# Two heads' score products side by side, and the gate products moved into the attention, in a two-block transformer kernel

## The reference, cut to what matters

```
mod = silu(c) @ w_ada + b_ada ; mod_c = silu(c_ctx) @ w_ada + b_ada
hx, hc = modulate(rmsnorm(x)), modulate(rmsnorm(ctx))
qa, ka, va, qb, kb, vb, ga, gb = project(hx)      # w_in, heads of 64, q and k normed per head
ka, va, kb, vb of hx (with rotary embedding) and of hc are concatenated: 512 keys
ya = softmax(qa ka^T / 8) va                      # 8 query heads, 2 key heads (grouped)
yb = (softmax(q1 k1^T / 8) - lam * softmax(q2 k2^T / 8)) vb    # 4 heads, two halves of 64 each
yb = rmsnorm(yb per head) * subln * 0.8
x  = x + g_a * ((sigmoid(ga) * (ya @ w_oa) + sigmoid(gb) * (yb @ w_ob)) @ w_out)
x  = x + g_m * moe(modulate(rmsnorm(x)))          # router, 32 experts, top 4
```

## Time and profile before

| | |
|---|---|
| median of 3 runs | 2022.0 us (2020.96 to 2022.55) |
| span of the profiled execution | 2021.8 us |
| first block up to the expert loop | 0 to 412.4 us |
| of it: projections / second part of the modulation / attention | 46.3 to 202 / 202 to 231 / 231 to 319.5 us |
| expert loop | 412.4 to about 1425 us |
| TensorE busy | 1822.9 us, 90% |

### The profile page before, as it was taken

One profiled execution on the slowest core, in us unless ns is written; L12 is line 12 of the kernel. 1 busy time (PEld: TensorE's weight loads), 2 busy tenths in 40 slices (PEclk: granted clock), 3 DMA queues, 4 the chain that ended last, 5 costly groups with the idle time before them and its releaser, 6 DMA issues.

```text
span 2021.8 us, 18937 instructions
## 1 busy us (share of the span) xinstructions
PE 1822.9 (90%) x7644; PEld 951.9 (47%) x7644; DVE 379.6 (19%) x806; ACT 318.8 (16%) x612; POOL 35.5 (2%) x35
## 2 busy tenths in 40 slices
PE   4999868799989899898998989989699999989997
PEld 2558336433324233242332423324477788768743
DVE  1330353311101111111111111111312221211001
ACT  2111341110101101011010110101133222010000
POOL 0110000000000000000000000000100000000000
PEclk8999999899989899999999999999899999999999
DMA  9533812279899898998989989899433324334410
GB/s 370 193 112 138 335 42 68 107 289 426 350 406 429 328 426 348 422 427 354 429 362 419 427 356 430 360 420 414 165 115 125 125 105 144 127 125 166 154 55 21
DMA packets 86609, 536.66 MB, mean 265 GB/s; under 512 B 4544, under 2 KB 5696, under 8 KB 61984
## 3 DMA queue, kind: packets, MB, share of 16 engines
q1 hardware_dynamic: 84720, 530.60, 65.2%
q10 hardware_dynamic: 1840, 5.38, 0.7%
HBM read 534.91 MB, written 1.05 MB: 265 GB/s over the span
## 4 chain that ended last, share of the span: by engine, by line
PE 76%; issue 13%; DVE 5%; DMA 2%; ACT 2%; DVEq 1%; SPq 0%; POOL 0%; ACTq 0%; POOLq 0%
PE ps L1513 34%; PE ps L1250 25%; PE ps L1517 4%; PE ps L1489 3%; PE ps L1530 2%; DMA ring<-in_w_ada 2%; ACT arena L581 1%; DVE arena L1041 1%; DVE arena L1037 1%; DVE stat L868 1%; PE ps L1546 1%; PE ps L1405 1%; PE ps L1263 1%; DVE arena L1028 1%; SPq L295 0%
## 5 line engine op out<-in xcount | busy, mean ns | idle before, releaser
L1513 PE MATMUL ps<-ring,arena 128*64 128x512 f32 x3072 | 706.9, 615 | 23.0 <-ACT arena L581 23.0
L1513 PEld LDWEIGHTS ps<-ring,arena 128*64 128x64 f32 x3072 | 222.5, 142 | 473.1 <-issue 442.2
L1250 PE MATMUL ps<-arena,ring 128*128 128x256 f32 x1856 | 408.2, 381 | 2.5 <-ACT arena L621 2.0
L1250 PEld LDWEIGHTS ps<-arena,ring 128*128 128x128 f32 x1856 | 353.6, 191 | 51.9 <-ACT arena L621 2.6
L1250 PE MATMUL ps<-ring,arena 128*128 128x512 f32 (+1 forms) x480 | 195.3, 564 | 4.5 <-issue 3.4
L1250 PEld LDWEIGHTS ps<-ring,arena 128*128 128x128 f32 x480 | 90.2, 190 | 100.4 <-issue 97.2
L1032 DVE TENSOR_SCALAR arena<-ps 128x512 f32<-128x512 f32 x32 | 22.1, 692 | 498.0 <-PE ps L1517 498.0
L1756 PE MATMUL ps<-ring,arena 128*128 128x512 f32 x256 | 110.0, 592 | 0.0
L1517 PE MATMUL ps<-arena 128*64 128x512 f32 x384 | 98.6, 592 | 0.0
L1756 PEld LDWEIGHTS ps<-ring,arena 128*128 128x128 f32 x256 | 48.6, 190 | 60.8 <-issue 60.7
L1530 PE MATMUL ps<-arena 128*128 128x512 f32 x128 | 62.9, 618 | 15.8 <-ACT arena L588 10.9
(11 more groups left out here) (223 smaller groups left out, 938.9 us busy)
## 6 DMA issues: line engine op xcount, KB each, us to landing
ring<-in_w_up SPq DMA_DIRECT2D x72, 2048.0 KB, 13.6
ring<-in_w_down SPq DMA_DIRECT2D x72, 2048.0 KB, 9.9
ring<-in_w_gate SPq DMA_DIRECT2D x64, 2048.0 KB, 11.6
ring<-in_w_in SPq DMA_DIRECT2D x23, 2048.0 KB, 10.7
ring<-in_w_ada SPq DMA_DIRECT2D x12, 2048.0 KB, 9.9
ring<-in_w_out SPq DMA_DIRECT2D x4, 2048.0 KB, 15.7
ring<-in_w_branch SPq DMA_DIRECT2D x3, 2048.0 KB, 7.7
ring<-in_w_oa SPq DMA_DIRECT2D x1, 2048.0 KB, 17.5
```

The costliest lines, as they stand in the source:

```text
L1250: last = pe.matmul(dst, a, b, start=k == 0, stop=k == len(terms) - 1)
L1513: last = pe.matmul(dst[CAP * g:CAP * g + CAP, :], stationary(half, c), w[:, c, 512 * g:512 * g + 512], start=half == 0 and c == 0, stop=False)
```

## The change

- `QA` and `QB` hold two heads in one column, one in rows 0 to 63 and one in rows 64 to 127 (no zeros, no memset of GpSimd). `scores_pair` issues two score products, each over 64 rows, into two banks. Four banks hold scores; two banks the transposed probabilities, one the products with V, and bank 7 the gates.
- The eight gate products leave the projections. Four are issued in attention steps 2, 6, 10, 14 and four in steps 16, 18, 20, 22, after the score products and before the wait for the probabilities. ScalarE copies each result out of the bank between `pt_out` and `pv_out`, and takes the sigmoid of all eight behind the attention.
- Projections run in the order K, Q, V, and the blocks of weights with them; the eight modulation blocks come before the gates.
- The transposed probabilities lie in the context half of `hT` and beside it, since the gate products still read the other half.
- The outputs of the differential attention are copied to `obuf`, and one head norm takes all eight; their eight transposes lie between the second and the third product with `w_oa`. `w_oa` is loaded in two halves of 64 rows.
- Four semaphores of small loads become one, waited for at 64 by VectorE where it waited for the row vector before.

```diff
+W_ADA1, W_KVA, W_KB, W_QA, W_QB, W_VB, W_ADA2 = 0, 4, 5, 6, 7, 8, 9
+W_GATE, W_OA, W_OB, W_OUT, W_MOE = 17, 21, 22, 23, 25
...
+        def gate_fill(k):
+
+            return k // 4 if k < 16 and k % 4 == 2 else 4 + (k - 16) // 2 if k in (16, 18, 20, 22) else None
...
-            pool.memset(area(4096, 4096), 0.0).then_inc(sem("q_zeroed"), 1)
...
-            for i in range(8):
-                inverse_root(brs[:, i:i + 1])
+            inverse_root(brs)
...
+                    act.activation(obuf[:, v - 4, :], bank(6, P), ACT.Copy).then_inc(sem("pv_read"), 1)
                     act.drain()
-                    act.activation(squares[:, v % 2, :], bank(6 + v % 2, P), ACT.Square,
+                    act.activation(squares[:, v - 4, :], obuf[:, v - 4, :], ACT.Square,
...
+                if gate_fill(k) is not None:
+                    s = gate_fill(k)
+                    act.wait_ge(sem("gate_done"), s + 1)
+                    act.activation(sig[:, s, :], bank(7), ACT.Copy).then_inc(sem("gate_read"), 1)
...
+            act.drain()
+            for s in range(8):
+                act.activation(sig[:, s, :], sig[:, s, :], ACT.Sigmoid).then_inc(sem("sig_ready"), 1)
+            for half in range(2):
+                act.wait_ge(sem("ybt_done"), half + 1)
+                act.activation(ybT[:, 2 * half:2 * half + 2, :].rearrange("p c q -> p (c q)"), bank(4 + half), ACT.Copy,
+                               scale=sub08).then_inc(sem("ybt_read"), 1)
...
+            dve.wait_ge(sem("bss_done"), 8)
+            inverse_rms(brs, bss, P, SUBLN_EPS)
+            dve.drain()
+            dve.tensor_tensor(obuf, obuf, brs.unsqueeze(2).broadcast_to([P, 8, P]), ALU.mult).then_inc(sem("on_done"), 1)
...
+            def gate_product(s):
+                i, part = W_GATE + s // 2, s % 2
+                if s:
+                    pe.wait_ge(sem("gate_read"), s)
+                ready(i)
+                w = wq_view(i)
+                for c in range(2):
+                    c0 = T * part + P * c
+                    last = product(bank(7)[:, T * c:T * c + T],
+                                   [(w[:, j, c0:c0 + P], hT[:, j, 0:T]) for j in range(KC)])
...
+            def scores_pair(n):
+                if n >= 4:
                     pe.wait_ge(sem("ex_done"), n - 2)
+                for r in range(2):
+                    rows = slice(64 * r, 64 * r + 64)
+                    if n < 16:
+                        h, qt = n // 4, (n // 2) % 2
+                        last = pe.matmul(bank((n + r) % 4), QA[rows, h, P * qt:P * qt + P], KTA[rows, :], start=True,
+                                         stop=True)
...
+                last.then_inc(sem("sc_done"), 2)
...
+            for k in range(24 + 1):
                 last_n = k if k < 16 else 17 + 2 * (k - 16)
                 while issued < min(last_n + 3, 32):
-                    scores(issued)
-                    issued += 1
+                    scores_pair(issued)
+                    issued += 2
+                if gate_fill(k) is not None:
+                    gate_product(gate_fill(k))
```

More of the change, by code:

```diff
@@ L889, in normalise @@
                                              prob[:, (n + 1) % 4, :], ALU.mult, ALU.subtract).then_inc(sem("pn_done"), 1)
[L891 to L898, removed]
             maxes(0)
-            for k in range(24 + 3):
+            for k in range(24):
                 if k + 1 < 16:
@@ L1320, in _ @@
                 dst = bank(s % 4)
[L1321 to L1334, removed]
-                                       [(w[:, j, c0:c0 + P], hT[:, j, 0:T]) for j in range(KC)])
-                    if part == 1:
-                        used()
-                last.then_inc(sem("proj_done"), 1)
-                if 2 <= s < 18 and UNIT[s - 2] is not None:
-                    qk_transpose(UNIT[s - 2])
-            pe.wait_ge(sem("proj_read"), 24)
+                i, cols, tile = steps[s]
+                ready(i)
+                w = wq_view(i, cols)
+                last = product(dst[:, 0:cols], [(hT[:, j, P * tile:P * tile + P], w[:, j, :]) for j in range(KC)])
+                if s == 15 or steps[s + 1][0] != i:
+                    used()
+                last.then_inc(sem("proj_done"), 1)
+                if 2 <= s < 14:
+                    qk_transpose(s - 2)
+            def gate_product(s):
+                i, part = W_GATE + s // 2, s % 2
+                if s:
+                    pe.wait_ge(sem("gate_read"), s)
+                ready(i)
+                w = wq_view(i)
[3 more added lines that the diff above has]
+                                   [(w[:, j, c0:c0 + P], hT[:, j, 0:T]) for j in range(KC)])
+                if part == 1:
+                    used()
+                last.then_inc(sem("gate_done"), 1)
+            pe.wait_ge(sem("proj_read"), 16)
             for n in range(4, 12):
@@ L1368, in weighted_a @@
                 pe.wait_ge(sem("pt_read"), 4 * c + 4)
-                if c >= 2:
-                    pe.wait_ge(sem("ya_read"), c - 1)
-                g = c // 2
+                if c:
+                    pe.wait_ge(sem("pv_read"), c)
                 for kc in range(4):
-                    for hh in range(2):
-                        last = pe.matmul(bank(6 + c % 2, T)[64 * hh:64 * hh + 64, :], VA[:, kc, 64 * g:64 * g + 64],
-                                         PTA[:, 2 * (c % 2) + hh, kc, :], start=kc == 0, stop=kc == 3)
+                    for g in range(2):
+                        last = pe.matmul(bank(6, T)[64 * g:64 * g + 64, :], VA[:, kc, 64 * g:64 * g + 64],
+                                         pta(2 * (c % 2) + g)[:, kc, :], start=kc == 0, stop=kc == 3)
                 last.then_inc(sem("pv_done"), 1)
```

199 lines of the change are left out of this document (94 added, 105 removed).

## The result

The changed kernel takes 2029.1 us (median of 8 runs, 2025.0 to 2034.4) against 2021.6 (8 runs, 2019.9 to 2024.5): ratio 1.0037, 95% interval 1.0027 to 1.0048. It is 0.4% slower; 0.7% faster was forecast, and the time lies outside the range. The profiled execution took 2030.3 us, its span is 2028.5.

What follows compares the result with a forecast made beforehand. TensorE was taken to bound the projections, engines taking turns the attention, and the expert loop to stay fixed. Terms -55.3 + 29.5 + 7.9 + 1.3 + 2.5 = -14.1 gave 2007.7 span, 2008 us median; range 1999 to 2019.

Steps and rivals of the forecast that it cites:

- The step that failed: Expert loop, 1012.6 us: none of its instructions changes, so only the first 412 us of the kernel can change.
- Rival 2: Attention: the clock falls more often, four or more half-clock stretches, gate products under them; +4 to +8, 2012 to 2016; chance 0.13.
- The list of signs: Whole kernel: what traces would show if right or wrong, such as projections 55 us shorter or stages behind 412 us changing time.
- The sum for the first block: Stages up to 412 us: -55.3 + 29.5 + 7.9 + 1.3 + 2.5 = -14.1 us.
- Projections: Projections before the attention: eight gate products of 6.91 us leave TensorE's path, -55.3 us.
- First part: First 16 attention steps: four gate products hide only 0.3 us each; 69.7 in place of 40.2 us, +29.5.
- The score pair: Attention scores: two products over 64 rows run side by side in 0.86 us, 1.13 with both turns.
- Rival 1: Attention scores: the two row halves run one behind the other; +13, 2020 to 2021 us; chance 0.12.
- Second part: Last eight attention steps: four gate products stand where TensorE waited for VectorE; 56.0 in place of 48.1 us, +7.9.
- 2.5 for the clock: Attention: 1.5 half-clock stretches taken, between bounds of none and four, each costing 1.7 us where TensorE is full; +2.5.
- Table: Router behind the attention: its exponential must load its own table again, 1.28 us on the path; +1.3.
- Head norm, weights: One norm, 3.6 to 5 us, is covered by two `w_oa` products, 7.0; gate weight loads are hidden; nothing added.

## Why the prediction was wrong, by its own steps

**The step that failed** is the one that set the frame: "none of its instructions changes. Only the first 412 us can." The instructions didn't change, and their time did, by +15.6 us. The row that spoke against the step was among those read: a clock of 0.96 in the loop. I priced half-clock stretches in the attention, where I saw them cost 1.7 us each, and took the same loss in the loop as fixed, though it was some 32 us there (1017.9 against 986.0 with the pauses filled) and hung on where the pauses fall against the clock's changes. Rival 2 had the clock fall more often; in the attention it came true (below), but it didn't look behind 412 us. The list of signs did name one, that the stages behind 412 us might not keep their time, without a price. Cut into its eight groups, the loop of the kernel before would have shown 127.8, 129.5 and 129.6 once each and 126.3 five times for the same work, and so that anything from 8 x 126.3 = 1010 to 8 x 129.65 = 1037 us was open, 8 us down and 19 up. (The windows of the earlier trace rows end at 1425, some 5 us before the loop does.)

In the loop the clock was 0.50 to 0.69, in windows of 3.4 us, behind pauses of 2 to 3 us, and 1.00 with the pauses filled: 1018 and 1033 us against 986. Not every such pause is followed by a fall: behind the one of 2.0 us before the second expert's transposes the clock stays at 1.00 in a short group (1099.45 to 1102.85 in the kernel before).

**The sum for the first block**, term by term, in this pair of profiles:
- *Projections:* -55.3, measured -56.6. The wait for the last modulation block stayed, 15.33 us on the chain in both. The 1.3 us more are the clock's: around the end of that wait it stands at half for 6.8 us in the kernel before and for 3.4 in the changed one, and the stretch from the wait's end to the first score product takes 7.54 us against 6.21.
- *First part:* 69.7 us to the transposes of step 16, measured 70.1 (174.68 to 244.75). Right in each step: 15.0 us a period, ScalarE waiting under each gate product.
- *The score pair:* 0.86 taken, 1.06 with the turns.

```profile
264.65 1.13 PE L1253 MATMUL ps<-arena 128*128 128x128 f32 x8 [0.51 <-ACT arena L519]
265.71 1.13 PE L1366 MATMUL ps<-arena 64*128 64x512 f32 x4
270.21 0.91 PE L1407 MATMUL ps<-const,arena 128*128 128x128 f32 x4 [3.38 <-DVE arena L898]
```

  Two products over 64 rows (x4) take 1.13 where one over 128 rows took 1.02; 1.06 from the start of a pair to the gate product behind it (180.51 to 181.57). The two products of a pair start within 0.01 us of each other. Rival 1 falls. For the two turns of a pair the trace shows 1.06 less 0.86, 0.2 us, where 0.27 were taken, so it isn't the pairs that made the kernel slower.
- *Second part:* mis-sized. From the transposes of step 16 to the end of the `w_ob` products it took 91.7 us (244.75 to 336.41) against 76.0 before (271.44 to 347.42), +15.7, where 7.9 and 2.5 for the clock were forecast. Two causes: four half-clock stretches with 17.1 us in all, one in each step without a gate product, as in this window,

```profile
251.50:255.00 3.50, 3.50 (x14) 3.04 (x16) 0.00 (x0) 0.60 (x1) 0.00 (x0) 0.50 0.00 0
```

  where 1.5 of 3.4 us were taken (four were the upper bound); and a wait that I missed: with one bank for the results with V, `weighted_b` waits for ScalarE's copy of the last one, which stands behind the gate product in ScalarE's queue ([0.51 <-ACT arena L519] above). That wait is 0.68 us at each of three steps, 2.0 us at most. The other 3 us of the error are left for the clock; no run measured them by themselves.
- *Table:* +1.3, measured +1.17 from the end of the `w_ob` products to the loop. ScalarE loads it for 1.28 us at 386.73 and goes on at 388.02.
- *Head norm, weights:* nothing, as forecast; the third `w_oa` product follows the eight transposes without a wait (the piece at 315.69).

-9.8 up to the loop, against -14.1. Over all profiles the saving is smaller still, some 5.4 us (see the filled pauses), and the changed kernel's first block stands longer at half clock; so the clock was the mis-sized term of this sum too.

## What to carry to other kernels

Here the time of the stage behind a pause of TensorE wasn't fixed (7.09 or 10.07 us for the same 32 instructions behind the same pause of 2.0), and a loop that repeats the same pauses held on to a pattern for most of its laps, a good one (seven of 126.3 us) or a bad one (seven of 129.65). So a saving of some microseconds, read from one pair of profiles, can be off by as much as here (9.8 in one pair, 5.4 in the mean). Before a change of 10 us is judged, cut every long loop into laps and look whether laps of the same work differ; if they do, fill the pauses in both versions and compare those. Filling them was worth having by itself (25 us in the kernel before), and work that is moved to cover waits belongs where the same queue waits, not where another queue must then wait for it: four gate products moved from the first part to the second took off 19.6 us.

## What the runs showed of the hardware

- 2.0 us of memsets on the way into a loop of 1018 us moved the whole time by +20 us in one kernel, and by -15 in the other, whose loop took 1033; laps had one of three lengths, 123.3, 126.3 or 129.65 us, and no others but one of 127.8 or 127.9 at the entry of two profiles.
- Three dummy matmuls (2.6 us at 0.86 each) in a pause of 2.9 cost nothing that could be seen, since a lap of 123.3 us at full clock occurs without them too, and with those in the other pauses they kept the clock at 1.00; the whole gained some 25 us in the kernel before and 43 in the changed one.
- Profiled and other executions of one kernel can differ by over 1%: 2018 twice under the profiler, 2042 to 2044 in four runs without. That the pattern makes the difference wasn't shown.
